# Top-k search packed into the query stage, ScalarE's exponential and ids parted, transposes in the norms, weights split three units ahead

## The chip, the core and the metric

The kernel runs on one core of one Trainium2 chip. The metric is the device time of one execution in microseconds; of several executions the median is taken. A core has TensorE (PE; PEld is its weight load), the vector engine (DVE), ScalarE (ACT), GpSimd (POOL) and SyncE (SP, which here only issues DMAs). Each engine works through its own list of instructions in order and waits on semaphores.

## What is computed

A two-layer encoder over 256 tokens of width 1024, all in float32. Each layer is a token mixer (windowed attention in layer 0, spatial gating in layer 1) and a product-key expert mixer, each behind an RMS norm and added to the residual. The expert mixer is what the change touches:

```python
def peer(h, w_query, sub_keys, expert_down, expert_up):
    q = (x @ w_query).reshape(T, PEER_HEADS, 2, D_HALF)          # 8 heads
    s = jnp.einsum('thcd,hckd->thck', q, sub_keys)
    s1, i1 = lax.top_k(s[:, :, 0], 16)
    s2, i2 = lax.top_k(s[:, :, 1], 16)
    cand = s1[..., :, None] + s2[..., None, :]
    cidx = i1[..., :, None] * 128 + i2[..., None, :]
    top_s, pos = lax.top_k(cand.reshape(T, 8, 256), 16)
    idx = jnp.take_along_axis(cidx.reshape(T, 8, 256), pos, axis=-1)
    gate = jax.nn.softmax(top_s, axis=-1)
    a = gelu(einsum('cd,chkd->chk', x, expert_down[idx]))
    y = einsum('chk,chkd->cd', a * gate, expert_up[idx])
```

There are 128 x 128 = 16384 experts. The kernel does not gather their rows: it multiplies by all of them and uses a table of gates that is zero but for the chosen ones.

## The kernel before

**Units.** All weights are streamed through SBUF in units of 128 x 1024 floats (512 KB). SyncE loads unit n into `raw[n % 4]` once `split_lo(n - 4)` is done (L282). ScalarE rounds it to fp32r in `w_hi[n % 4]` (`split_hi`, L451) and the vector engine forms the rest in `w_lo[n % 4]` (`split_lo`, L674). TensorE multiplies with three products, hi x hi, lo x hi and hi x lo (L1154 to L1156). `split_hi(n)` waits until TensorE has used unit n - 4 (`used >= n - 3`). The split of a unit stands AHEAD = 2 units ahead of its use in every engine's program.

**Stages of a layer.** The mixer (20 units in layer 0, 72 in layer 1), a norm, the query stage (16 units), the down stage (128 units, `acts` = gelu of x times all experts' down rows), the up stage (128 units), and the residual. In the norm (`norm_turn`, L1186) TensorE transposes the scaled activations, ScalarE copies them to `x_hi` and the vector engine forms `x_lo`.

**The search.** An item is one head of one tile of 128 tokens, 16 items a layer. Its top-k runs on the vector engine in small steps that are placed by hand between the weight splits: `sides_first`, `sides_places`, `sides_second`, `sides_last` (top 16 of each half), `candidates`, `best_first` to `best_last` (top 16 of the sums), `best_parts`, `best_columns`, `best_hits`, `best_keys`, `best_experts` (ids in `chosen`, semaphore `found`), `same_*` (an expert that was chosen by an earlier head too), `totals` (the gate in `whole`, semaphore `gate_done`). In the query stage, iteration c of the vector engine is the split of unit c + AHEAD, a copy of the scores of unit c (which TensorE finishes behind unit c + 1) and the steps that stand under `if c == ...`. In the down stage every item has a slot of SLOT = 7 units; the slot of item m also holds the last steps of item m - 1. ScalarE does `exponentials(item)` (waits `shifted`, which `best_parts` sets) and `names(item)` (waits `found`, writes the scatter's addresses, sets `named`); it stands in its own loop behind the eviction of a unit. After the exponential it loads the Gelu table again (L600).

**The scatter.** GpSimd first clears the table `gates` in DRAM by 32 DMAs of zeros a layer (L370); in layer 0 the last 8 wait for the first 8 query units. Then it stores the gates by indirect DMAs, 16 an item and 256 a layer (L385):

```python
for m in range(ITEMS):
    pool.wait_ge(gate_done, ITEMS * layer + m + 1)
    pool.wait_ge(named, ITEMS * layer + m + 1)
    if head:
        pool.wait_ge(added[layer][t], 16 * TOPK * head)
    for k in range(TOPK):
        pool.indirect_dma_start(flat, ...)
```

**The up stage.** SyncE's order there is the load of up unit 0, then a wait until all stores of the layer have landed (`added`, L312), then the gates of column 0 into `g_t`, up unit 1, and so on. For each column the vector engine multiplies `acts` by `g_t` (`gate`, L1113), ScalarE rounds the product to `l_hi` (`operand_hi`, L639, which waits until TensorE has used the unit before the last), the vector engine forms `l_lo` (`operand_lo`, L1118), and TensorE uses both with the up unit (`rows`). In ScalarE's program `split_hi(up + c + AHEAD)` stands ahead of `operand_hi(c + 1)`. In the down stage it stands ahead of the eviction of column c (`evict`, L624).

## Time and profile before

| | before |
|---|---|
| median of 3 runs | 1984.69 us (1978.02 to 1987.01) |
| profiled execution, its own time | 1983.99 us |
| span of its instructions | 1982.2 us |
| mean granted TensorE clock | 0.98 |
| PE busy | 1878.9 us (95%) |
| DVE busy | 1376.1 us (69%) |
| ACT busy | 1009.6 us (51%) |
| POOL busy | 704.5 us (36%) |
| chain that ended last | PE 59%, POOL 26%, issue 8% |

The profile is of one execution. Times in its rows are microseconds from the first instruction; a granted clock of 1.00 is 2.4 GHz and 0.50 is 1.2 GHz. Matmul rows overlap, since their ends are modelled: the distance from start to start is the rate. In a timeline row "[2.49 <-DVE big L713]" says how long the engine had stood idle before the instruction and what released it. "xN" counts the instructions merged in a row.

### The profile page before, as it was taken

What the parts mean: (1) busy time and instruction counts of PE and PEld (TensorE: products, weight loads), DVE (VectorE), ACT (ScalarE), POOL (GpSimd) and SP (SyncE); (2) the same over time, 40 slices, a digit from 0 to 9 for tenths busy, and PEclk for the clock granted to TensorE, in tenths of its full rate; (3) what the DMA queues carried; (4) which work ended last, traced back from release to release, by engine and by line L of the source; (5) the groups of instructions that cost most, each with busy time, mean ns of one, the idle gap of its engine ahead of it and who ended that gap; (6) DMA issues with size and microseconds to landing.
All of it is one profiled execution on the core that took longest, in us unless ns stands there. A gap on an engine that the chain in (4) does not pass through costs nothing.

```text
span 1982.2 us, 38591 instructions
## 1 busy us (share of the span) xinstructions
PE 1878.9 (95%) x12066; PEld 1706.5 (86%) x12066; DVE 1376.1 (69%) x2944; ACT 1009.6 (51%) x1633; POOL 704.5 (36%) x628
## 2 busy tenths in 40 slices
PE   7989999999959999999999999999999959999998
PEld 6889999999958888887889989999999948888886
DVE  5857778887436667667577767778888427766666
ACT  5634565665435555555444445565565425555553
POOL 1314777888730000000102103778788740000000
PEclk9989999999979999999999999999999979999999
DMA  6974555545547778886849744545555537777775
GB/s 226 343 253 168 177 164 181 176 167 180 188 131 242 240 242 280 290 295 213 280 153 335 268 145 156 182 161 181 176 172 173 192 106 240 242 241 241 240 241 194
DMA packets 158145, 419.96 MB, mean 212 GB/s; under 512 B 32267, under 2 KB 65067, under 8 KB 157580
## 3 DMA queue, kind: packets, MB, share of 16 engines
q1 hardware_dynamic: 129116, 369.23, 56.5%
q0 software_dynamic: 28976, 50.17, 7.6%
q8 instruction: 16, 0.26, 0.1%
q14 instruction: 37, 0.30, 0.0%
HBM read 382.30 MB, written 37.00 MB: 212 GB/s over the span
## 4 chain that ended last, share of the span: by engine, by line
PE 59%; POOL 26%; issue 8%; ACT 2%; DVE 2%; DMA 2%; SPq 0%; DVEq 0%; POOLq 0%; ACTq 0%
POOL gates L385 26%; PE psum L1154 19%; PE psum L1156 19%; PE psum L1155 19%; DMA big<-bias_rows 1%; PE psum L1335 1%; ACT w_hi L451 1%; DVE w_lo L674 1%; PE psum L1312 1%; ACT L600 1%; DVE big L713 1%; ACT L598 0%; PE psum L1239 0%; PE psum L1265 0%; DMA raw<-in_up 0%
## 5 line engine op out<-in xcount | busy, mean ns | idle before, releaser
L674 DVE TENSOR_TENSOR w_lo<-raw,w_hi 128x1024 fp32r<-128x1024 f32 x636 | 772.0, 1219 | 257.7 <-ACT w_hi L451 256.9
L1154 PE MATMUL psum<-x_hi,w_hi 128*128 128x256 f32 x2576 | 739.8, 287 | 19.3 <-DVE w_lo L674 16.6
L1155 PE MATMUL psum<-x_lo,w_hi 128*128 128x256 f32 x2576 | 732.1, 284 | 0.0
L1156 PE MATMUL psum<-x_hi,w_lo 128*128 128x256 f32 x2576 | 731.8, 284 | 0.0
L385 POOL DMA_INDIRECT gates<-whole,address x512 | 629.1, 1229 | 253.4 <-issue 165.0
L451 ACT CAST w_hi<-raw 128x1024 fp32r<-128x1024 f32 x636 | 661.2, 1045 | 60.4 <-DMA raw<-in_up 49.9
L1154 PEld LDWEIGHTS psum<-x_hi,w_hi 128*128 128x128 f32 x2576 | 497.5, 193 | 30.0 <-issue 28.2
L1155 PEld LDWEIGHTS psum<-x_lo,w_hi 128*128 128x128 f32 x2576 | 497.9, 193 | 0.9
L1156 PEld LDWEIGHTS psum<-x_hi,w_lo 128*128 128x128 f32 x2576 | 497.5, 193 | 0.0
L1154 PE MATMUL psum<-w_hi,l_hi 128*128 128x512 f32 x1152 | 453.5, 394 | 45.7 <-DVE l_lo L1118 44.6
L1156 PE MATMUL psum<-w_hi,l_lo 128*128 128x512 f32 x1152 | 450.2, 391 | 0.0
L1155 PE MATMUL psum<-w_lo,l_hi 128*128 128x512 f32 x1152 | 450.1, 391 | 0.0
L1154 PEld LDWEIGHTS psum<-w_hi,l_hi 128*128 128x128 f32 x1152 | 217.5, 189 | 90.5 <-issue 46.4
L639 ACT CAST l_hi<-big 128x256 fp32r (+1 forms) x256 | 104.1, 406 | 336.7 <-PE psum L1156 333.1
L624 ACT ACTIVATE big<-psum 128x256 f32<-128x256 f32 x256 | 97.9, 382 | 324.7 <-PE psum L1156 324.7
L1156 PEld LDWEIGHTS psum<-w_hi,l_lo 128*128 128x128 f32 x1152 | 217.3, 189 | 45.9
L1155 PEld LDWEIGHTS psum<-w_lo,l_hi 128*128 128x128 f32 x1152 | 217.5, 189 | 44.7
L1118 DVE TENSOR_TENSOR l_lo<-big,l_hi 128x256 fp32r<-128x256 f32 x256 | 109.0, 426 | 211.1 <-ACT l_hi L639 210.9
L437 POOL DMA_DIRECT2D big<-h_kept x4 | 2.2, 554 | 366.4 <-PE psum L1156 366.4
L370 POOL DMA_DIRECT2D gates<-zeros x64 | 48.3, 756 | 198.0 <-PE psum L1156 188.3
L1113 DVE TENSOR_TENSOR big<-big,g_t 128x256 f32 (+1 forms) x256 | 107.1, 419 | 2.9 <-DMA g_t<-gates 2.8
L425 POOL DMA_DIRECT2D big<-in_ln_g x4 | 2.2, 549 | 209.3 <-PE psum L1156 209.3
(134 smaller groups left out, 1116.4 us busy)
## 6 DMA issues: line engine op xcount, KB each, us to landing
raw<-in_down SPq DMA_DIRECT2D x256, 512.0 KB
raw<-in_up SPq DMA_DIRECT2D x256, 512.0 KB
raw<-in_sg_units SPq DMA_DIRECT2D x72, 512.0 KB
gates<-zeros POOLq DMA_DIRECT2D x64, 512.0 KB, 6.2
g_t<-gates SPq DMA_DIRECT2D x256, 128.0 KB, 3.7
raw<-in_query SPq DMA_DIRECT2D x32, 512.0 KB
raw<-in_attn_units SPq DMA_DIRECT2D x20, 512.0 KB
gates<-whole,address POOLq DMA_INDIRECT x512
```

What stands on the lines that cost most here:

```text
L370: pool.dma_start(gates[layer][ZERO_UNITS * q:ZERO_UNITS * q + ZERO_UNITS].rearrange("i p t -> p i t"), zeros[:, :].rearrange("p (o t) -> p ...
L385: pool.indirect_dma_start(flat, bass.IndirectOffsetOnAxis(address[:, TOPK * m + k:TOPK * m + k + 1], 0), whole[:, t, head, k:k + 1], None, ...
L451: act.copy(w_hi[n % SPLIT][:, :], raw[n % RAW][:, :]).then_inc(hi_done, 1)
L600: act.preload_act_table(ACT.Gelu_apprx_tanh)
L624: act.activation(acts[:, bass.ds(i * group + n, 1), :], p1[n % 2].rearrange("p (o t) -> p o t", o=1), ACT.Gelu_apprx_tanh).then_inc(p1_rea ...
L639: act.copy(l_hi[n % 2][:, :].rearrange("p (o t) -> p o t", o=1), acts[:, bass.ds(i * GROUP + n, 1), :]).then_inc(l_hi_done, 1)
L674: dve.tensor_tensor(w_lo[n % SPLIT][:, :], raw[n % RAW][:, :], w_hi[n % SPLIT][:, :].bitcast(F32), ALU.subtract).then_inc(lo_done, 1)
L1113: dve.tensor_tensor(a, a, g_t[n % G_TILES][:, :].rearrange("p (o t) -> p o t", o=1), ALU.mult).then_inc(gated_up, 1)
L1118: dve.tensor_tensor(l_lo[n % 2][:, :].rearrange("p (o t) -> p o t", o=1), acts[:, bass.ds(i * GROUP + n, 1), :], l_hi[n % 2][:, :].bitcast ...
L1154: pe.matmul(out_ap, hi_s, hi_m, start=start, stop=False)
L1155: pe.matmul(out_ap, hi_s, lo_m, start=False, stop=False)
L1156: return pe.matmul(out_ap, lo_s, hi_m, start=False, stop=stop)
```

## The change

It makes six edits.

1. AHEAD goes from 2 to 3: every split, in all stages, is placed one unit earlier against TensorE's use.
2. In the query stage the steps are packed. Item 0's gate (`totals(0)`) goes from iteration 13 to 7, item 1's from the down stage to iteration 12, and item 2's search is done up to `best_columns`. Item 3's sides are started in iteration 15 and finished in the first two units of the down stage. The slots of the down stage begin at unit 2 (SLOTS_FROM) with item 3 (FIRST_ITEMS), and end at unit 100 and not 105.
3. On ScalarE `exponentials` and `names` are parted: in the query stage they stand behind units 7 and 8 for item 0, and 12 and 13 for item 1; in a slot, behind its first and third unit.
4. The Gelu table is no longer loaded in `exponentials` but behind it, and not between items 0 and 1.
5. The second, third and fourth `norm_turn` begin with FILL = 26 transposes of old `x_lo` columns into PSUM bank 7, and nothing reads what they write. They wait for nothing.
6. A tile `iota` that nothing used is gone, so `made` counts to 7 and not to 8 (those lines are left out below).

```diff
--- before.py
+++ after.py
@@ -33,7 +33,10 @@
 CAND = WIDE * TOPK + (TOPK - WIDE) * NARROW
 HALF = NK // 2
 SLOT = 7
+SLOTS_FROM = 2
+FIRST_ITEMS = 3
 ZERO_UNITS = 4
+FILL = 26
 G_TILES = 4
 RMS_EPS, LN_EPS = 1e-6, 1e-5
 MASKED = -1.0e30
@@ -44,7 +47,7 @@
 GROUP = 4
 RAW = 4
 SPLIT = 4
-AHEAD = 2
+AHEAD = 3
 ATTN_UNITS, SG_V_UNITS, SG_UNITS, QUERY_UNITS = 20, 24, 72, 16
 MIX_UNITS = (ATTN_UNITS, SG_UNITS)
 SG_LOADS = 16
...
@@ -597,7 +596,6 @@
                     act.wait_ge(shifted, ITEMS * layer + item + 1)
                     act.activation(vals[:, item % 2, :], top1[:, item % 2, :], ACT.Exp, bias=least[:, item % 2:item % 2 + 1],
                                    accum_out=sums[:, item % 2:item % 2 + 1]).then_inc(exp_done, 1)
-                    act.preload_act_table(ACT.Gelu_apprx_tanh)
 
                 def names(item):
 
@@ -613,10 +611,15 @@
                     split_hi(u["query"] + c + AHEAD)
                     act.wait_ge(used, u["query"] + c + 1)
                     act.copy(q_p[c % 2], p1[c % 2]).then_inc(p1_read, 1)
-                    if c == 9:
+                    if c == 7:
                         exponentials(0)
+                    if c == 8:
+                        names(0)
                     if c == 12:
-                        names(0)
+                        exponentials(1)
+                        act.preload_act_table(ACT.Gelu_apprx_tanh)
+                    if c == 13:
+                        names(1)
 
                 def evict(n, i=0, group=GROUP):
 
@@ -624,12 +627,16 @@
                     act.activation(acts[:, bass.ds(i * group + n, 1), :], p1[n % 2].rearrange("p (o t) -> p o t", o=1),
                                    ACT.Gelu_apprx_tanh).then_inc(p1_read, 1)
 
-                for n in range(SLOT * (ITEMS - 1)):
+                searched = SLOTS_FROM + SLOT * (ITEMS - FIRST_ITEMS + 1)
+                for n in range(searched):
                     split_hi(u["down"] + n + AHEAD)
                     evict(n)
-                    if n % SLOT == 2:
-                        exponentials(n // SLOT + 1)
-                        names(n // SLOT + 1)
+                    item = (n - SLOTS_FROM) // SLOT + FIRST_ITEMS - 1
+                    if n >= SLOTS_FROM and (n - SLOTS_FROM) % SLOT == 0:
+                        exponentials(item)
+                        act.preload_act_table(ACT.Gelu_apprx_tanh)
+                    if n >= SLOTS_FROM and (n - SLOTS_FROM) % SLOT == 2:
+                        names(item)
 
                 def operand_hi(n, i=0):
 
@@ -639,7 +646,7 @@
                     act.copy(l_hi[n % 2][:, :].rearrange("p (o t) -> p o t", o=1),
                              acts[:, bass.ds(i * GROUP + n, 1), :]).then_inc(l_hi_done, 1)
 
-                for n in range(SLOT * (ITEMS - 1), NK):
+                for n in range(searched, NK):
                     if n == SCORES_COLUMN:
                         act.wait_ge(search_done, layer + 1)
                         act.wait_ge(h_stored, 16 * (layer + 1))
...
@@ -1016,55 +1023,72 @@
                                     pg[c % 2][:, 0:T].rearrange("p (t n) -> p t n", t=TT)).then_inc(s_read, 1)
                     if c == 2:
                         a = sides_first(0)
+                        a = sides_places(0, a)
                     if c == 3:
-                        a = sides_places(0, a)
-                    if c == 4:
                         a = sides_second(0, a)
                         a = sides_last(0, a)
+                        b = candidates(0, a)
+                    if c == 4:
+                        b = best_first(0, b)
+                        b = best_places(0, b)
+                        b = best_second(0, b)
+                        b = best_last(0, b)
                     if c == 5:
-                        b = candidates(0, a)
-                        a = sides_first(1)
-                    if c == 6:
-                        b = best_first(0, b)
-                        a = sides_places(1, a)
-                    if c == 7:
-                        b = best_places(0, b)
-                        a = sides_second(1, a)
-                    if c == 8:
-                        b = best_second(0, b)
-                        a = sides_last(1, a)
-                        b = best_last(0, b)
-                    if c == 9:
                         b = best_parts(0, b)
                         b = best_columns(b)
+                        e = best_hits(b)
+                    if c == 6:
+                        e = best_keys(e)
+                        best_experts(e)
+                    if c == 7:
+                        totals(0, None)
+                        a = sides_first(1)
+                        a = sides_places(1, a)
+                    if c == 8:
+                        a = sides_second(1, a)
+                        a = sides_last(1, a)
+                        b = candidates(1, a)
+                    if c == 9:
+                        b = best_first(1, b)
+                        b = best_places(1, b)
+                        b = best_second(1, b)
+                        b = best_last(1, b)
                     if c == 10:
-                        b = best_hits(b)
-                        b = best_keys(b)
+                        b = best_parts(1, b)
+                        b = best_columns(b)
+                        e = best_hits(b)
                     if c == 11:
-                        best_experts(b)
-                        b = candidates(1, a)
+                        e = best_keys(e)
+                        best_experts(e)
                         a = sides_first(2)
                     if c == 12:
-                        b = best_first(1, b)
+                        totals(1, None)
                         a = sides_places(2, a)
                     if c == 13:
-                        totals(0, None)
-                        b = best_places(1, b)
+                        a = sides_second(2, a)
+                        a = sides_last(2, a)
+                        b = candidates(2, a)
                     if c == 14:
-                        b = best_second(1, b)
-                        a = sides_second(2, a)
-                        b = best_last(1, b)
+                        b = best_first(2, b)
+                        b = best_places(2, b)
+                        b = best_second(2, b)
+                        b = best_last(2, b)
                     if c == 15:
-                        b = best_parts(1, b)
-                        a = sides_last(2, a)
+                        b = best_parts(2, b)
                         b = best_columns(b)
+                        a = sides_first(3)
 
                 def low(n):
 
                     split_lo(u["down"] + n + AHEAD)
 
-                for item in range(2, ITEMS + 1):
-                    n = SLOT * (item - 2)
+                a = sides_places(3, a)
+                low(0)
+                a = sides_second(3, a)
+                a = sides_last(3, a)
+                low(1)
+                for item in range(FIRST_ITEMS, ITEMS + 1):
+                    n = SLOTS_FROM + SLOT * (item - FIRST_ITEMS)
                     now, more = item < ITEMS, item + 1 < ITEMS
                     e = best_hits(b)
                     if now:
@@ -1103,7 +1127,8 @@
                     if now:
                         b = best_columns(b)
                 dve.sem_inc(search_done, 1)
-                for n in range(SLOT * (ITEMS - 1), NK):
+
+                for n in range(SLOTS_FROM + SLOT * (ITEMS - FIRST_ITEMS + 1), NK):
                     low(n)
 
                 def gate(n, i=0):
@@ -1185,6 +1210,9 @@
 
             def norm_turn(z):
 
+                if z:
+                    for k in range(FILL):
+                        pe.transpose(psum[:, 7, P * (k % 4):P * (k % 4) + P], x_lo[:, k % KD, 0:P].bitcast(F32), ident[:, :])
                 for t in range(TT):
                     pe.wait_ge(scaled_done, TT * z + t + 1)
                     for k in range(KD):
```

## Rows read from the trace of the kernel before

**Rows 1.** The page, chain that ended last, share of the span by engine.
```profile
PE 59%; POOL 26%; issue 8%; ACT 2%; DVE 2%; DMA 2%; SPq 0%; DVEq 0%; POOLq 0%; ACTq 0%
```

**Rows 2.** Windows: stretch, length, busy PE, PEld, DVE, ACT, POOL, clock, DMA share, GB/s.
```profile
120.00:173.00 53.00, 51.48 (x424) 50.53 (x424) 32.82 (x101) 21.88 (x37) 7.35 (x9) 1.00 0.64 219
173.00:556.00 383.00, 374.55 (x3080) 370.39 (x3078) 281.92 (x739) 217.50 (x360) 304.25 (x248) 1.00 0.52 172
556.00:576.00 20.00, 0.14 (x2) 0.00 (x0) 2.40 (x5) 2.27 (x4) 8.02 (x9) 0.61 0.36 113
```

**Rows 3.** Waits: engine and line, waited for whom: us, times, longest.
```profile
POOL gates L385 <- DVE whole L1006: 87.8, 2, 60.9
...
PE psum L1154 <- DVE l_lo L1118: 44.6, 2, 24.7
```

**Rows 4.** Timeline, first gate, first and last store of layer 0, first of layer 1.
```profile
170.60 0.23 DVE L1006 TENSOR_SCALAR whole<-vals,sums 128x16 f32<-128x16 f32 x1
...
171.69 1.97 POOL L385 DMA_INDIRECT gates<-whole,address  x1 [26.91 <-DVE whole L1006]
...
565.50 0.96 POOL L385 DMA_INDIRECT gates<-whole,address  x1 [0.30 <-issue]
...
1214.46 2.03 POOL L385 DMA_INDIRECT gates<-whole,address  x1 [60.89 <-DVE whole L1006]
```

**Rows 5.** Timeline of ACT: query units 0, 8, 12, ids; layer 1's unit 8.
```profile
120.67 0.37 ACT L615 COPY big<-psum 128x256 f32<-128x256 f32 x1 [3.04 <-PE psum L1156]
...
148.10 0.37 ACT L615 COPY big<-psum 128x256 f32<-128x256 f32 x1 [3.03 <-PE psum L1156]
...
163.42 0.37 ACT L615 COPY big<-psum 128x256 f32<-128x256 f32 x1 [2.96 <-PE psum L1156]
...
163.93 0.30 ACT L609 ACTIVATE address<-big,token 128x16 uint32<-128x16 f32 x1
...
1189.33 0.37 ACT L615 COPY big<-psum 128x256 f32<-128x256 f32 x1 [3.16 <-PE psum L1156]
```

**Rows 6.** Source L370, the clear issued at 144.03.
```profile
DMA to landing us min/median/max: 5.0/5.0/5.0
```

**Rows 7.** Windows around two norms, columns as in rows 2.
```profile
115.50:120.00 4.50, 4.44 (x21) 4.47 (x22) 3.40 (x7) 2.13 (x5) 0.00 (x0) 0.50 0.00 0
...
926.70:929.50 2.80, 0.01 (x1) 0.00 (x0) 2.45 (x7) 1.18 (x4) 1.63 (x2) 0.91 0.52 180
929.50:932.40 2.90, 2.87 (x14) 2.87 (x15) 0.75 (x1) 0.43 (x2) 0.01 (x1) 0.50 0.00 0
```

**Rows 8.** Timeline of PE, four transposes at the full clock.
```profile
59.85 0.60 PE L1239 MATMUL psum<-ident,big 128*128 128x128 f32 x4
```

**Rows 9.** Source L385 in 500 to 550, then in 556 to 567: ns min/median/max.
```profile
L385 POOL DMA_INDIRECT gates<-whole,address x35: 954/1151/1320, 499.4 to 549.6; - x35
...
L385 POOL DMA_INDIRECT gates<-whole,address x9: 954/958/959, 555.4 to 565.5; - x9
```

**Rows 10.** Timeline of SP's queue, ACT and PE, handoff of layer 0.
```profile
568.07 0.42 SPq L282 DMA_DIRECT2D raw<-in_up  x1
...
569.01 0.43 SPq L282 DMA_DIRECT2D raw<-in_up  x1
...
572.39 1.04 ACT L451 CAST w_hi<-raw 128x1024 fp32r<-128x1024 f32 x1 [18.70 <-DMA raw<-in_up]
...
576.07 0.77 PE L1154 MATMUL psum<-w_hi,l_hi 128*128 128x512 f32 x1 [19.93 <-DVE l_lo L1118]
```

**Rows 11.** Timeline of ACT, second weight split of the program.
```profile
9.64 1.05 ACT L451 CAST w_hi<-raw 128x1024 fp32r<-128x1024 f32 x1 [0.81 <-DMA raw<-in_attn_units]
```

**Rows 12.** Timeline of DVE, residual behind layer 0's up stage.
```profile
924.79 2.65 DVE L713 TENSOR_TENSOR big<-psum,big 128x512 f32<-128x512 f32 x4 [0.29 <-PE psum L1156]
```

**Rows 13.** Timeline of ACT and DVE, one unit of the up stage.
```profile
703.80 0.41 ACT L639 CAST l_hi<-big 128x256 fp32r x1 [1.36 <-PE psum L1156]
...
704.24 0.43 DVE L1118 TENSOR_TENSOR l_lo<-big,l_hi 128x256 fp32r<-128x256 f32 x1 [0.82 <-ACT l_hi L639]
```

12 lines of the change are left out of this document (4 added, 8 removed).

## The prediction

> **What bounds the kernel now.** I read the chain that ended last first, because a busy share averages over stages with different limits. TensorE and GpSimd's indirect stores at L385 divide that chain [rows 1]. The windows by stage say where. In a down stage TensorE is busy 374.55 of 383 us, so its own rate nearly sets the length. Then it does nothing for 20.0 us, while the vector engine and ScalarE do 2.4 and 2.3 us of work and GpSimd goes on scattering [rows 2]. The waits put this idle time and layer 1's, which is 24.7 us (44.6 us together), down to the first `l_lo` of the up stage. They also show that GpSimd waited for a gate only twice in 512 stores, once a layer, before the first store [rows 3]. So the search does not pace the scatter. From its first store at 171.69 to the end of its last at 566.46, 394.8 us, it never lacks work [rows 4]: 256 stores at 1.54 us. A scatter that starts x earlier ends x earlier, and until 20 us are won the up stage starts x earlier. What makes the down stage itself faster moves nothing; it only lengthens TensorE's wait. The change has to be read in this order: what starts the scatter, what its stores cost, what follows the last one.
>
> **Start of the scatter.** Item 0's first store needs `gate_done`, `named` and the cleared `gates`. Today the gate is computed in iteration 13 of the query stage and the ids named in iteration 12. After the change they are computed in iterations 7 and 8. What ends last then? ScalarE's names(0) run right behind the copy of unit 8. Before, that copy began at 148.10, and unit 12's at 163.42 with the last of the three id activations ending at 164.23, so 0.8 us behind that copy's start [rows 5]. If nothing else moved, the ids would be ready at 148.9. The vector engine must have the gate by then. Work for one item is, from the trace, about 7 us (the sixteen iterations hold 32.8 us of vector work [rows 2], of which 16 x (1.13 + 0.34) = 23.5 us are weight splits and score copies; the 9.3 us left hold all of item 0 and half of items 1 and 2, with waits between dependent steps outside the busy time). Packed, each iteration holds 1.47 us of split and copy and 1.6 to 1.7 us of search, 3.1 to 3.2 us in all, against 3.39 us for a TensorE unit here (27.43 us from unit 0's copy to unit 8's, over 8, gives 3.43 [rows 5]). It fits with little room, and the third split unit covers an iteration that overruns. Following the new order from iteration 2 on gives the gate of item 0 about 3.9 us after unit 7's end, ahead of the names. The cleared `gates`: the last clear is issued at 144.03, behind unit 7, and lands 5.0 us later [rows 6], so 0.4 us behind the names at most. From readiness to the first store the trace shows 0.86 us (gate computed at 170.60 in 0.23 us, store at 171.69 [rows 4]).
>
> **The clock and the fill.** TensorE's granted clock is 0.50, its lower level of 1.2 GHz, from 115.5 to 120.0, the first query unit of layer 0 [rows 7], and so it is in layer 1; before that TensorE had stood idle for the norm. 26 transposes at the full clock take 26 x 0.107 = 2.8 us (four take 0.60 us with 0.27 us of pipeline behind the last [rows 8]), no more than the idle time of the tightest of the three norms, 2.8 us between the layers [rows 7]; the other two have 3.5 and 3.8. They wait for nothing and so cost nothing, and if the clock stays at its upper level, the first query unit is paced by `x_lo` instead: it ends 0.8 us behind the last `x_lo`. The norm's sixteen transposes end sooner too. Together that is 3.0 us earlier in layer 0 (1.0 of it from the transposes), 2.1 us in layer 1 by the same reckoning (its transposes began at the full clock), and 0.9 us at the norm between the layers. Do fp32 transposes hold the clock? In 929.5 to 932.4 TensorE ran transposes alone, at the lower level, and from 932.4 on it stood at the upper one [rows 7]. Here transposes raised it. The Trainium skill says otherwise ("TensorE: Matmul & The Clock Gate", Part 4, PE-mode transpose: transposes do not count as TensorE activity for the clock in the same way). By that rule of the Trainium skill the fill would be worth nothing and the sum 6.0 us higher; the trace disagrees with it at 932.4. I go by the trace, with a doubt that is priced as a rival.
>
> **Start of the scatter, summed.** Layer 0: unit 8 ends 3.0 earlier, at 145.1; names at 145.9; first store at 146.8, 24.9 us earlier. Layer 1: unit 8's copy began at 1189.33 [rows 5]; less 2.1, plus 0.8 and 0.86, gives 1188.9, plus 0.4 (below) against 1214.46 [rows 4], 25.2 us earlier. The Exp table in layer 1 is loaded behind unit 7's copy and is done (1.28 + 0.5 us) before unit 8 ends.
>
> **Cost of a store.** With the vector engine idle a store takes 0.96 us, all nine from 556 to 567; behind the search, with one weight split a unit, they range from 0.95 to 1.32 [rows 9]. So one split costs the scatter 0.36 us. Starting five query units earlier, it meets 5 more splits, 1.8 us, and one more item's search, about 1 us (bounds 0 and 3). Items 0 and 1 took 48.2 us together, and item 2's gate comes about 48.5 us after the first store (15 units at 2.88 to 3.4 us, and 3.1 us of split and steps), so a short wait of 0 to 1.5 us appears; I take 0.7. Sum 3.5 us a layer, bounds 1 and 10 (the upper end: items 0 and 1 at 1.7 us a store, the dearest item's mean of 27.4 us). The Trainium skill ("SBUF — State Buffer", Who interferes with whom) infers that `tensor_tensor` does not hold up descriptor generation; by it this term would be 0.7 us, and the trace disagrees by its 0.36 us a split.
>
> **Handoff to the up stage.** SyncE stands behind the `added` wait with only up unit 0 loaded. Unit 1 was issued at 568.07 and landed for ScalarE at 572.39; then split, the last eviction, both gates and `l_hi`, `l_lo` led to TensorE at 576.07, 3.7 us later [rows 10]. With AHEAD 3, ScalarE must also split up unit 2 before it evicts column 127, and unit 2 is issued at 569.01. By bytes (1.3 MB at some 300 GB/s) it lands at about 573.8. So +1.4 us a layer, bounds 0.9 (the issue alone) and 3.
>
> **What else AHEAD moves.** At the start a third split stands ahead of the copy of the bias row and of `x_hi`. The second began at 9.64 after a wait of 0.81 for its weights [rows 11], and the third's land about 1.6 us behind it (0.5 MB at some 340 GB/s): +1.7 us, bounds 1.0 and 3, since bias_rows goes on to DMA and to the first scores. At the end of layer 0's up stage the last split now waits for unit 126 and ends at about 926.3, so the residual starts there and not at 924.79 [rows 12]: +1.4 us, less 0.9 for the clock, +0.5. At the end of the gating stage the same costs 0.4. In the up stage ScalarE's split (1.05 us) now waits for the same unit as `l_hi` and goes first. `l_lo` started 0.44 us behind `l_hi` (703.80, 704.24) and takes 0.43; with the split ahead it is ready 1.9 us after the unit's end, where 2.72 us are to be had [rows 13]. Covered, so nothing; without that cover each 0.1 us late would be 25.6 us over 256 units.
> The 15 slots of each down stage lose 0.55 to 0.8 us each to ScalarE's two table loads (8.4 us of idle TensorE in 383 [rows 2]); the third unit hides them. It wins 8 to 12 us a layer for TensorE and nothing for the end, because the scatter ends later. Dropping `iota` (0.25 us of GpSimd at the start) is behind the DMA of `x`: nothing.
>
> **Sum.** Start +1.7. Layer 0: -24.9 + 3.5 + 1.4 = -20.0. Between layers +0.5. Layer 1: -25.2 + 3.5 + 1.4 = -20.3. Together -38.1 us. The profiled execution took 1983.99 us (span 1982.2 and 1.8 around it), 0.7 below the median of 1984.69: 1983.99 - 38.1 = 1945.9, rounded 1946. TensorE would still idle 17 us in layer 0 (down stage ends at 539.4, up starts at 556.1, both less the 1.7) and about 21 us in layer 1.
>
> **Rivals.** (1) The fill does not hold the clock: the first query units stay at the lower level, +3.0, +2.1, +0.9 = 1952. Against it stands 932.4 [rows 7]; for it, some idle time remains behind the fill and behind the norm's transposes. The Trainium skill's rule on transposes, named above, is this case. (2) The scatter slows: the vector engine is nearly full from iteration 2 on, every split and search step holds up stores, and item 2's gate is just late. +6 us a layer: 1958. (3) The packed search overruns: if an iteration takes over 3.43 us on average, the third unit's reserve is gone after a few, TensorE stalls and the first store slips by some iterations. Losing half of the advance gives 1971. (4) Less contention than I charge and a handoff that costs nothing: 1938. (5) The other side: `l_lo` in the up stage. Behind the split it has 0.8 us of room. From 2.72 us on TensorE waits in each of 256 units; at 0.15 us beyond, the whole gain is eaten, at 0.2 us a unit it ends at 1946 + 51 = 1997. The 1.9 us from [rows 13] speak against it. (6) The change does not do what it says: the clears or another wait hold the first store where it was, and the extra unit's costs remain, 1984 + 5 - 6 = 1983.
>
> **Chances.** Forecast 0.52 (own range 1940 to 1950), rival 1 0.18, rival 2 0.11, rival 3 0.05, rival 4 0.06, rival 5 0.05, rival 6 0.03. Faster than before by over 0.5% (about what a measurement here can tell from no change) in all but rivals 5 and 6: 0.92, of which I move 0.02 to no change for what I have not seen; same 0.05, slower 0.05. The range takes in the forecast and rivals 1, 2 and 4: 1936 to 1960.
>
> **What would show it.** First store at about 148.5 in layer 0 (146.8 + 1.7) with its wait ending on the names; stores without idle time but for item 2; the clock at its upper level through the norms; no 0.55 us gaps in the down stage; TensorE idle 17 and 21 us before the up stages, ended by `l_lo`; up units still 2.72 us. A first store behind 155 us, gaps in the query stage, or up units over 2.8 us would make the prediction wrong.

## The result and the profile after

The changed kernel took 1965.40 us (median of 4, 1962.08 to 1965.82), the kernel before in the same comparison 1985.85 us (4 runs): a ratio of 0.9896, 95% interval 0.986 to 0.9932. The forecast was 1946 us, in 1936 to 1960, so the time lies above the range. The change won 20 us and not 38. The profiled execution took 1965.82 us, with a span of 1963.7 us.

In four of the later comparisons the kernel before itself took 2239 to 2291 us (medians); no execution time from those is used in the argument.

The chain that ended last, of the page of the changed kernel, answers to [rows 1]:

```profile
PE 58%; POOL 28%; issue 8%; DMA 2%; DVE 1%; ACT 1%; SPq 0%; DVEq 0%; POOLq 0%; ACTq 0%
```

GpSimd's share has grown from 26 to 28%. The windows of the down stage of layer 0 and of the two idle times before the up stages, in the columns of [rows 2]:

```profile
173.00:541.00 368.00, 368.00 (x3069) 368.00 (x3068) 276.28 (x708) 214.53 (x349) 292.47 (x227) 1.00 0.58 177
541.30:569.70 28.40, 0.00 (x0) 0.00 (x0) 3.63 (x6) 3.60 (x6) 13.40 (x14) 0.55 0.27 93
...
1576.90:1606.00 29.10, 0.00 (x0) 0.00 (x0) 3.65 (x6) 3.62 (x6) 13.41 (x14) 0.59 0.27 90
```

TensorE now has 368.00 us of work in 368 of down stage: the gaps of the slots are gone. It then stands idle for 28.4 and 29.1 us, where it was 20.0 and 24.7. The third unit ahead did for TensorE what it should and the end got nothing of it, as forecast; but the waits were to shrink to 17 and 21 us. The waits of the changed kernel, as in [rows 3]:

```profile
POOL gates L384 <- issue: 168.6, 510, 3.9
...
PE psum L1179 <- DVE l_lo L1143: 57.7, 2, 29.2
...
POOL gates L384 <- ACT address L607: 35.3, 1, 35.3
...
POOL gates L384 <- DMA gates<-zeros: 5.1, 1, 5.1
```

The up stages wait for `l_lo` for 57.7 us in all. GpSimd waits for another engine or a DMA only ahead of its first store of a layer (for the clears in layer 0, for the ids in layer 1). Under "issue" the row also holds two pauses a layer, of 3.3 to 3.9 us, before the 113th and the 225th store (at 338.0 and 517.7 in layer 0). The kernel before has them at the same two stores, 1.7 to 4.0 us long. What they wait for the profile doesn't name. The first and last stores of both layers, timeline, which answer to [rows 4]:

```profile
149.82 1.63 POOL L384 DMA_INDIRECT gates<-whole,address  x1 [5.09 <-DMA gates<-zeros]
...
557.85 0.96 POOL L384 DMA_INDIRECT gates<-whole,address  x1 [0.31 <-issue]
...
1184.92 1.74 POOL L384 DMA_INDIRECT gates<-whole,address  x1 [35.31 <-ACT address L607]
...
1593.41 0.96 POOL L384 DMA_INDIRECT gates<-whole,address  x1 [0.30 <-issue]
```

The first store of layer 0 is 21.9 us earlier, the last one only 7.6 (565.50 to 557.85). The scatter took 409.0 us in layer 0 and 409.4 in layer 1, where it had taken 394.8 and 399.9. A store's mean length rose from 1.225 and 1.233 us in the two layers to 1.268 and 1.270. In layer 0 that makes 11.0 us, and the two pauses another 3.2; in layer 1 it makes all of the 9.5.

From the two traces, each term of the sum against what it measured (positions of the first or last store, of TensorE's first product of a stage, and of the ends of spans):

| term | forecast | measured |
|---|---|---|
| start (TensorE's last attention unit, 104.72 to 107.96) | +1.7 | +3.2 |
| first store, layer 0, against that | -24.9 | -25.1 |
| scatter, layer 0 | +3.5 | +14.2 |
| handoff (end of the last store to TensorE), layer 0 | +1.4 | +1.3 |
| up stage, residual, norm | +0.5 | +0.8 |
| gating stage to first store, layer 1 | -25.2 | -24.0 |
| scatter, layer 1 | +3.5 | +9.5 |
| handoff, layer 1 | +1.4 | +2.3 |
| up stage of layer 1 to the end | 0 | -0.8 |
| sum | -38.1 | -18.6 |

The measured column adds up to the difference of the spans, 1982.2 - 1963.7 = 18.5. Of the 19.5 us that are missing, 16.7 lie in the scatter. Each column of positions is one execution.

### The profile page after: what moved, and what is told of

Same layout as the page of the kernel before. It is cut to its first block, busy times and chain, and to the rows that moved or that the text cites. A ratio compares the mean times of both kernels' runs of the same rounds, so it can differ in the third digit from the quotient of the medians.

```text
span 1963.7 us, 38730 instructions
## 1 busy us (share of the span) xinstructions
PE 1869.4 (95%) x12144; PEld 1706.1 (87%) x12144; DVE 1381.6 (70%) x2944; ACT 1006.9 (51%) x1629; POOL 725.0 (37%) x627
## 4 chain that ended last, share of the span: by engine, by line
PE 58%; POOL 28%; issue 8%; DMA 2%; DVE 1%; ACT 1%; SPq 0%; DVEq 0%; POOLq 0%; ACTq 0%
POOL gates L384 28%; PE psum L1179 18%; PE psum L1181 18%; PE psum L1180 18%; DMA big<-bias_rows 1%; PE psum L1363 1%; PE psum L1340 1%; DMA raw<-in_up 1%; DVE big L720 1%; PE psum L1267 0%; PE psum L1256 0%; PE psum L1293 0%; DMA raw<-in_attn_units 0%; ACT w_hi L450 0%; POOL stat L356 0%
## 5 line engine op out<-in xcount | busy, mean ns | idle before, releaser
L384 POOL DMA_INDIRECT gates<-whole,address x512 | 649.8, 1269 | 209.0 <-issue 168.6
L1179 PE MATMUL psum<-w_hi,l_hi 128*128 128x512 f32 x1152 | 453.4, 394 | 58.7 <-DVE l_lo L1143 57.7
```

The lines of the kernel that those rows point to most:

```text
L384: pool.indirect_dma_start(flat, bass.IndirectOffsetOnAxis(address[:, TOPK * m + k:TOPK * m + k + 1], 0), whole[:, t, head, k:k + 1], None, ...
L1179: pe.matmul(out_ap, hi_s, hi_m, start=start, stop=False)
```

## Why the scatter became slower: a first look

One stretch of the changed kernel's down stage, stores first, then the vector engine's steps with two SBUF operands (`tensor_tensor`) that ran beside them:

```profile
224.12 0.96 POOL L384 DMA_INDIRECT gates<-whole,address  x1 [0.30 <-issue]
225.38 0.96 POOL L384 DMA_INDIRECT gates<-whole,address  x1 [0.30 <-issue]
...
228.50 1.91 POOL L384 DMA_INDIRECT gates<-whole,address  x1 [0.30 <-issue]
...
232.41 2.53 POOL L384 DMA_INDIRECT gates<-whole,address  x1 [0.30 <-issue]
```

```profile
226.14 1.23 DVE L681 TENSOR_TENSOR w_lo<-raw,w_hi 128x1024 fp32r<-128x1024 f32 x1 [2.86 <-ACT w_hi L450]
...
228.36 1.22 DVE L681 TENSOR_TENSOR w_lo<-raw,w_hi 128x1024 fp32r<-128x1024 f32 x1
...
232.31 1.20 DVE L681 TENSOR_TENSOR w_lo<-raw,w_hi 128x1024 fp32r<-128x1024 f32 x1
233.43 0.68 DVE L994 TENSOR_TENSOR big<-big,whole 128x512 f32<-128x512 bf16 x1
...
234.52 1.23 DVE L681 TENSOR_TENSOR w_lo<-raw,w_hi 128x1024 fp32r<-128x1024 f32 x1
```

At 224.12 the vector engine has no step of the kind and the store takes 0.96 us. The store at 228.50 begins inside the split of 228.36 to 229.58 and takes 1.91. The one at 232.41 meets a split and the product of L994 back to back and takes 2.53. So a store's price is no constant 0.36 us per split; it hangs on where in the store the step falls and on what follows without a gap.

The traces let one say more. The split that began at 226.14, inside the store of 225.38, cost that store nothing. The two long stores end 0.83 us behind the end of the step, or of the row of steps without a gap, that ran when they began: 229.58 + 0.83 = 230.41, and 234.11 + 0.83 = 234.94. Of the 274 stores of the changed kernel that took over 1.0 us, 271 end 0.83 us behind the end of such a step, and in the kernel before 263 of 266. A split that begins after the store has begun leaves it at 0.96 us, 122 times in the changed kernel. So a store waits at its start, if such a step is running then, and not later.

**Theory A.** A store stops while the vector engine runs steps with two SBUF operands. Putting the splits one unit further ahead takes away the pauses in which stores ran free, so the same vector work costs more stores' time. **Theory B.** The early start in a crowded query stage and the new places of the steps make the scatter dearer, whatever AHEAD is. **Rival C**, tried later: any busy vector engine, or the streamed loads, slow the stores.

## Experiments

**AHEAD alone, undone and done.** Two kernels:

```diff
 # after_ahead2: the changed kernel
-AHEAD = 3
+AHEAD = 2
 # before_ahead3: the kernel before
-AHEAD = 2
+AHEAD = 3
```

> The changed kernel with AHEAD back at 2, all else as changed. Theory A (spacing): a store's cost hangs on how the vector engine's long two-input steps fall against it, and splitting three units ahead is what moved that from 14 to 12 stores in a 7-unit slot; then the scatter here takes about 395 to 400 us a layer (after: 409), the handoff 9.6 us (after: 11.0 and 11.7), the start loses 3 us less, and the time is about 1965 - 22 - 3 - 3 = 1937 us. Theory B (early start): the scatter is dearer because it begins in the crowded query stage and the steps of the slots were placed anew, whatever AHEAD is; then the scatter stays at 405 to 410 us and only start and handoff come back: about 1959 us. A third outcome, TensorE or the vector engine stalling in the query stage for want of the third unit, would show as a later first store (over 152 us).

Measured: 1944.35 us, ratio to before 0.9793 (0.9774 to 0.9812), that is 21 us below the changed kernel, which was measured in another comparison. The scatter takes 401.4 us in both layers (147.21 to 548.60 in layer 0). The handoff is 9.4 and 9.6 us, the first store comes 2.6 us earlier, and the query stage did not suffer. Windows of the down stage and of the two idle times:

```profile
173.00:545.80 372.80, 370.08 (x3054) 366.96 (x3052) 276.36 (x705) 216.01 (x351) 295.56 (x237) 1.00 0.57 175
545.80:558.00 12.20, 0.05 (x1) 0.00 (x0) 2.42 (x5) 2.29 (x4) 2.19 (x3) 0.70 0.58 194
1570.90:1583.10 12.20, 0.00 (x0) 0.00 (x1) 2.44 (x5) 2.31 (x4) 2.06 (x3) 0.65 0.57 207
```

The idle times are 12.2 us each. Most of the scatter's excess is gone: 409.2 us on average fell to 401.4, 7.8 less a layer, and a slot of seven units takes 20.53 us where it took 20.16. What stays against an average of 397.3 before is 4.1 us, near the 3.5 that the early start was priced at. Between the two traces, 22.1 us apart, 15.6 are the two scatters, 2.6 the start and 3.6 the two handoffs. Theory A had put the scatter at 395 to 400 us and Theory B at 405 to 410: the result lies just above A's range.

> The kernel before with AHEAD 3 and nothing else. Theory A: the 7-unit slots shrink from 20.96 to 20.16 us, stores per slot fall from 14 to 12 or 13, the scatter takes 405 to 410 us instead of 395 and 400; with +3 us at the start, +1.4 and +2 at the handoffs the time is about 1985 + 12 + 3 + 3 = 2003 us, though TensorE loses no time in the down stages. Theory B: the scatter keeps 395 to 400 us and the time is about 1991 us.

Measured: 1995.83 us, ratio 1.0044 (1.0028 to 1.0061): AHEAD 3 by itself makes the kernel slower by 9 us. But its scatter takes 398.8 and 399.0 us (394.8 and 399.9 before), as Theory B said, and not 405 to 410. TensorE's idle times before the up stages:

```profile
543.00:582.70 39.70, 0.01 (x1) 0.03 (x1) 3.69 (x6) 3.66 (x6) 21.06 (x22) 0.55 0.21 67
...
1598.50:1637.20 38.70, 0.01 (x1) 0.04 (x1) 3.71 (x6) 3.68 (x6) 21.08 (x22) 0.55 0.20 68
```

They are 39.7 and 38.7 us long, because in layer 0 TensorE ends its down stage 13 us earlier, while the scatter begins at 171.8 as before and ends 4 us later, and the handoff is 12.1 us and not 9.6. Stores in 220 to 420 us, the same 200 us of the down stage, in four kernels (before, changed, after_ahead2, before_ahead3), ns as min/median/max:

```profile
L385 POOL DMA_INDIRECT gates<-whole,address x129: 954/1118/2536, 218.7 to 418.8; - x129
```

```profile
L384 POOL DMA_INDIRECT gates<-whole,address x121: 954/1217/2935, 219.6 to 419.8; - x121
```

```profile
L384 POOL DMA_INDIRECT gates<-whole,address x123: 954/1179/2935, 219.7 to 418.5; - x123
```

```profile
L385 POOL DMA_INDIRECT gates<-whole,address x124: 955/1128/2872, 219.2 to 419.3; - x124
```

AHEAD 3 took the kernel before from 129 to 124 stores in that time. Over the two layers its scatter still grew by only 3 us. One part of that is seen: the down stage ended 27.6 us ahead of the end of the last store (10.3 before), and behind it stores cost 1.26 us from start to start and not 1.6. I estimate that at 5 us: the 17.3 us more of such a tail hold 13.7 stores, which at 1.6 us would take 22. Where the rest was won back isn't shown. Neither theory was right as put: AHEAD costs the scatter 7.8 us a layer in the new arrangement and next to nothing in the old one. Differences of 2 or 3 us a layer say little here, since `after_ahead2` and `ahead2_loads_first_3`, which have the same program up to the last store on all engines but SyncE, differ by 3.0 us in layer 1 (401.4 and 404.4).

**What a store waits for.** In the changed kernel the subtraction of each split (but for the first four units of each straight-line part) is replaced by a step that takes as long but reads one SBUF operand (and writes half as many elements). The low parts of the weights are left out of the result.

```diff
-dve.tensor_tensor(w_lo[n % SPLIT][:, :], raw[n % RAW][:, :], w_hi[n % SPLIT][:, :].bitcast(F32), ALU.subtract)
+dve.tensor_reduce(w_lo[n % SPLIT][:, 0:D // 2], raw[n % RAW][:, :].rearrange("p (n k) -> p n k", k=2), AX.X, ALU.add)
```

> The changed kernel with each weight split's subtraction replaced by a tensor_reduce of one SBUF operand (low parts of the weights left out), again, on a chip where the kernel before takes its usual 1985 us. Theory A (a store stops while a two-operand step of the vector engine runs): stores behind the search take 0.96 us, the scatter falls from 409 to 325 to 350 us a layer and the time to 1905 to 1920 us. Rival C (any busy vector engine, or the loads, slow the stores): scatter over 395 us, time about 1960 us.

Measured: 1907.39 us, in one execution. Stores in the same 200 us, and windows of the down stage and of what is left of the idle time before the up stage:

```profile
L384 POOL DMA_INDIRECT gates<-whole,address x152: 954/958/1934, 219.5 to 419.9; - x152
```

```profile
173.00:541.70 368.70, 368.69 (x3072) 368.48 (x3071) 278.59 (x715) 216.77 (x353) 238.21 (x238) 1.00 0.61 184
541.70:543.00 1.30, 0.00 (x0) 0.03 (x1) 0.95 (x4) 1.28 (x3) 0.00 (x0) 1.00 0.07 5
```

152 stores and not 121, with a median of 958 ns; the scatter takes 346.7 and 348.5 us; the vector engine is as busy as before (278.59 us of the stage) and the loads run as fast. Rival C is out. The run alone doesn't tell whether the second operand counts or the number of elements written, since the new step also writes half as many. The traces do: in nine of them (both kernels and the seven runs of this section outside its last table) a store began 142 times while a MATCH_REPLACE8 step ran, which reads one SBUF operand and writes as many elements as it reads, and none of these stores was lengthened. In this run 48 stores still take over 1.0 us, and 45 of them end 0.83 us behind another `tensor_tensor` step. Of the scatter's 346.7 and 348.5 us, 322 are 256 stores at 1.26 us, 10 and 13 are such longer stores, and 14 are pauses, 8 and 9 of them before the first store of item 2, whose gate now comes too late. With the scatter off the chain, TensorE waits 1.3 us before the up stage and its clock stays at the upper level.

**Shorter steps.** AHEAD 2, and each split's subtraction in two steps of 512 columns (indices shortened):

```diff
-dve.tensor_tensor(w_lo[:, :], raw[:, :], w_hi[:, :], ALU.subtract).then_inc(lo_done, 1)
+for b in range(2):
+    c = slice(D // 2 * b, D // 2 * b + D // 2)
+    ins = dve.tensor_tensor(w_lo[:, c], raw[:, c], w_hi[:, c], ALU.subtract)
+ins.then_inc(lo_done, 1)
```

> The changed kernel with AHEAD 2 and each split's subtraction in two steps of 512 columns, on a chip where the kernel before takes 1985 us. If a store waits for the running step alone: scatter 380 to 390 us a layer (401 with whole splits), time about 1920 us. If it waits until the vector engine has a pause: 1944 to 1950 us.

Measured: 1944.59 us, ratio 0.9774 (0.9747 to 0.9801), the same as with whole splits (0.9793); scatter 402.5 and 400.1 us.

```profile
L384 POOL DMA_INDIRECT gates<-whole,address x126: 952/1137/3006, 219.2 to 419.8; - x126
```

126 stores against 123 in that stretch, and nothing in the whole. The time is the one expected if a store waited until the vector engine has a pause, but the trace shows another reason. Of 89 stores that began inside the first half of a split, 60 ended 0.83 us behind that half and only 29 later, so a store mostly waits for the running half alone. One stretch with one split a unit, stores and then splits:

```profile
521.77 1.32 POOL L384 DMA_INDIRECT gates<-whole,address  x1 [0.31 <-issue]
523.39 0.96 POOL L384 DMA_INDIRECT gates<-whole,address  x1 [0.30 <-issue]
524.65 1.31 POOL L384 DMA_INDIRECT gates<-whole,address  x1 [0.30 <-issue]
```

```profile
520.96 1.29 DVE L683 TENSOR_TENSOR w_lo<-raw,w_hi 128x512 fp32r<-128x512 f32 x2 [1.59 <-ACT w_hi L450]
```

The store meets the second half and still waits 0.36 us, as with whole splits. Two stores take 2.52 us and a unit 2.88, so I take it that the stores drift against the splits until one of them meets a step late enough to lose just 0.36, whether the step is whole or halved. In all, the waits fell by 3.8 us a layer and the pauses between stores grew by 3.7.

**The handoff.** AHEAD 2, and all four buffers loaded before SyncE waits for the stores:

```diff
+for c in range(GROUP):
+    load(u["up"] + c, up_units[layer][:, bass.ds(c * D, D)], 0)
+
 def up_unit(c, i):
-    load(u["up"] + c, up_units[layer][:, bass.ds((i * GROUP + c) * D, D)], i)
+    if not isinstance(i, int):
+        load(u["up"] + c, up_units[layer][:, bass.ds((i * GROUP + c) * D, D)], i)
```

> The changed kernel with AHEAD 2 and up units 0 to 3 loaded before SyncE waits for the stores, on a chip where the kernel before takes 1985 us. Handoff 6.3 us and not 9.5: about 1938 us. If landing of the gates and the chain behind it take the time anyway: 1944 us.

Measured: 1935.73 us, ratio 0.9723 (0.9702 to 0.9743), the fastest version that keeps the whole computation; ahead of the changed kernel's 1965.40 by 30 us. Last store, gates' issue, and TensorE's first product of the up stage (timelines of POOL, SP and PE):

```profile
549.34 0.95 POOL L388 DMA_INDIRECT gates<-whole,address  x1 [0.30 <-issue]
...
551.54 1.75 SPq L321 DMA_DIRECT2D g_t<-gates  x4
...
555.06 0.77 PE L1183 MATMUL psum<-w_hi,l_hi 128*128 128x512 f32 x1 [7.85 <-DVE l_lo L1147]
```

The handoff is 4.8 us (550.29 to 555.06), 4.8 in layer 1 too, and not the 6.3 that was expected. The same edit with AHEAD 3 is among the runs that decide little, below.

**The fill.** The changed kernel without it, and the kernel before with it:

```diff
 # after_nofill: the changed kernel
-FILL = 26
+FILL = 0
 # before_fill: the kernel before, in norm_turn
+if z:
+    for k in range(26):
+        pe.transpose(psum[:, 7, P * (k % 4):P * (k % 4) + P], x_lo[:, k % KD, 0:P].bitcast(F32), ident[:, :])
```

> The changed kernel without the 26 transposes in the norms (FILL 0). If they hold the clock, the first unit behind each norm runs at 0.50 again here and the time rises by 3 to 6 us, to about 1970. If the clock stayed up for another reason (where the norm falls in time), it stays within 1 us of 1965.

> The kernel before with the 26 transposes at the start of norms 2, 3 and 4 and nothing else. If they hold the clock by themselves: granted clock 1.00 at the three norms, time 4 to 6 us less, about 1980. If they do not count as work for the clock: no difference.

Measured: without it 1971.36 us (ratio 0.9919, 0.9901 to 0.9937), 6.0 more than the changed kernel (4.6 by the two ratios to the kernel before, as the comparisons differ). With it alone 1982.50 against 1986.79 (0.9981, 0.9969 to 0.9994), 4.3 less. Windows of the norm's transposes and the first query unit in after_nofill, then of fill, transposes and first units in before_fill, clock in the third column from the end:

```profile
115.70:119.90 4.20, 3.64 (x16) 3.24 (x16) 1.69 (x4) 1.80 (x6) 0.27 (x1) 0.50 0.61 253
119.90:125.00 5.10, 5.01 (x23) 5.04 (x24) 3.42 (x7) 2.15 (x5) 0.00 (x0) 0.50 0.09 21
```

```profile
107.60:111.00 3.40, 2.78 (x26) 2.54 (x24) 2.65 (x7) 1.54 (x4) 1.61 (x3) 1.00 0.63 202
111.00:115.00 4.00, 2.66 (x22) 2.46 (x23) 2.51 (x7) 2.59 (x8) 0.36 (x2) 1.00 0.64 262
115.00:120.00 5.00, 5.00 (x43) 4.97 (x42) 2.64 (x5) 2.69 (x5) 0.76 (x1) 1.00 0.26 56
```

In after_nofill the clock is 0.50 where the changed kernel, of which it differs by the fill alone, has 1.00 (below); in before_fill it is 1.00 where the kernel before had 0.50 [rows 7]. It is the fill's transposes that keep the clock. In before_fill the stretches from TensorE's last product ahead of a norm to its fiftieth behind it are 2.9, 1.1 and 2.0 us shorter than in the kernel before, where 3.0, 0.9 and 2.1 were forecast.

**Runs that decide little.** They ran in the four comparisons in which the kernel before took over 2230 us. They are the edits above and two more (`after_loads_first`: the changed kernel with the four loads first; `after_half_stores`, `half_stores_2`: the changed kernel with every second store left out).

> The changed kernel with the low half of each weight split replaced by a tensor_reduce over the raw unit (from the fifth unit of each straight-line part and in all loops): the vector engine is as long busy, but reads one SBUF operand and not two. It leaves the low part of the weights out of the result. Theory A (a store stops while a long two-operand step of the vector engine runs, so the spacing of the splits sets its cost): stores behind the search all take 0.96 us (after: 0.95 to 1.32), a layer's scatter takes 322.6 us + what the search costs, 340 to 365 us (after: 409), and TensorE's wait before the up stage falls to a few us: about 1915 us. Rival C (the stores are slowed by any busy vector engine, or by DMA traffic of the streamed weights): the scatter stays above 395 us.

> The changed kernel with AHEAD 2 and the split's subtraction done as two steps of 512 columns. If a store waits for the running step alone, its wait is at most half as long: the scatter falls from 401 to 380 to 390 us a layer and the time from 1944 to about 1920 us. If a store waits until the vector engine has a pause, nothing changes but some 0.07 us more per split: 1944 to 1950 us.

> The changed kernel with AHEAD 2 and the loads of up units 0 to 3 issued before SyncE waits for the stores, so only the gates of column 0 stand between the last store and the up stage. The handoff from the last store to TensorE falls from 9.5 to about 6.3 us a layer: 1944 - 6.5 = 1938 us. If the landing of the gates and the chain gate, l_hi, l_lo is what takes the time anyway: 1944.

> The changed kernel with 8 of 16 stores per item; it leaves half of the gates out. If the scatter alone sets the two waits before the up stages, both vanish (28.5 and 29.2 us) and with them the lower clock behind them (2.6 us each): 1965 - 60 = about 1905 us. If something else then ends last before the up stage, a wait of several us remains and names it.

> The same kernel as in after_reduce_split (changed kernel, each weight split's subtraction replaced by a tensor_reduce of one SBUF operand, low parts of the weights left out), again, since there the kernel before itself took 2274 us and TensorE stood waiting for loads. There its stores took 0.96 us but for 0.3 us in all of a layer. Theory A: here too the stores take 0.96 us each, so a layer's scatter falls from 409 to 325 to 350 us, is done before the down stage ends or soon behind it, and the time is 1905 to 1920 us. Rival C (any busy vector engine, or the loads, slow the stores): scatter over 395 us.

> The same kernel as in ahead2_halves (changed kernel, AHEAD 2, each split's subtraction in two steps of 512 columns), again on another chip. If a store waits for the running step alone: scatter 380 to 390 us a layer (401 with whole splits), time about 1920 us. If a store waits until the vector engine has a pause: 1944 to 1950 us.

> The same kernel as in ahead2_loads_first (changed kernel, AHEAD 2, up units 0 to 3 loaded before SyncE waits for the stores), again on another chip. Handoff 6.3 us and not 9.5: about 1938 us. If landing of the gates and the chain behind it take the time anyway: 1944 us.

> The same kernel as in after_half_stores (changed kernel with 8 of 16 stores per item, half of the gates left out), again on another chip. If the scatter alone sets the waits before the up stages (28.5 and 29.2 us), they vanish and the time is about 1905 us; what is left of a wait names the next bound.

> The changed kernel as it is (AHEAD 3) with up units 0 to 3 loaded before SyncE waits for the stores. If the longer handoff of the changed kernel (11.0 and 11.7 us from the last store to TensorE) comes only from up unit 2 being loaded behind the wait, it falls to the 4.8 us that AHEAD 2 has with the same order, 13 us in all, and the time is about 1952 us, still 16 us above AHEAD 2 for the slower scatter (409 us a layer) and the later start. If the third split costs on ScalarE or the vector engine there, the handoff stays above 6 us. If the order of the loads also changes the scatter, it leaves 409 us.

> The same kernel as in after_loads_first (AHEAD 3, up units 0 to 3 loaded before SyncE waits for the stores), again, where the kernel before takes its usual 1985 us. If only the load of up unit 2 lengthened the handoff: handoff 4.8 us, scatter 409 us, about 1952 us. If the third split costs more there: handoff over 6 us.

| run | us | kernel before beside it |
|---|---|---|
| after_reduce_split | 2434.07 | 2274.36 |
| reduce_split_2 | 2424.70 | 2291.39 |
| ahead2_halves | 2308.41 | 2274.36 |
| ahead2_halves_2 | 2294.28 | 2291.39 |
| ahead2_loads_first | 2270.68 | 2274.36 |
| ahead2_loads_first_2 | 2282.68 | 2291.39 |
| after_half_stores | 2040.54 | 2274.36 |
| half_stores_2 | 2046.59 | 2291.39 |
| after_loads_first | 2265.32 | 2281.14 |
| after_loads_first_2 | 2220.05 | 2239.53 |

None of the expected times came, and none can be held against them: the kernel before itself is 250 to 305 us longer here than in every other comparison. What made it so is open. The traces show where it lies: in reduce_split_2 ScalarE stands idle some 15.5 us once in every slot, before the first eviction behind the Gelu load (254.6, 291.4, 328.6 and so on), while TensorE issues single products with gaps that the profile puts under "issue". It isn't the length of the stores, since the reduce_split runs, whose stores are short, are the longest. But it seems to hang on how many there are: the two runs with half of the stores are over 230 us shorter than the kernel before beside them, where taking the scatter off the chain was worth 82 us in reduce_split_3, and ScalarE's longest stops there are 4.3 to 4.9 us. That reduce_split took 1907.39 us in the one undisturbed run and 2424.70 and 2434.07 here says that its time rests on a single execution; the length of its stores doesn't, as their median is 0.96 us in all three. Whether the early loads help with AHEAD 3 wasn't settled. With half of the stores TensorE waits 1.3 us before either up stage, so the scatter is then off the chain.

## Why the prediction was wrong, point by point

**Bound and its reading: right.** The scatter, from its first store on, set the start of both up stages; closing TensorE's gaps won nothing by itself: with AHEAD 3 alone the down stage of layer 0 is 13 us shorter and the kernel 9 us slower. That the scatter "never lacks work" is not quite so, as it has the two pauses a layer named above.

**Start of the scatter: right.** -24.9 forecast and -25.1 measured in layer 0, -25.2 and -24.0 in layer 1. The gate came 3.7 us behind unit 7's copy (3.9 forecast), the names 0.8 us behind unit 8's. The sign that the first wait ends on the names came true in layer 1 only: in layer 0 the last clear, issued at 143.97, took 5.6 us to land, 0.8 us behind the names (0.4 at most forecast). No wait came at item 2, for which 0.7 us were summed: items 0 and 1 took 51.1 us and not 48.2, and its gate was ready 2.3 us before. With AHEAD 2 the wait is 2.2 us. A TensorE unit is given once as 3.39 us and once as 3.43 in that working; nothing hangs on it. In layer 1 a gap of 3.5 us in the gating stage, which had passed at the upper level before, was followed by 3.4 us at the lower one, about 1.7 us. So rivals (3) and (6) are out: the packed search fits, and the first store moved.

**Fill and clock: right (rival 1 is out).** 6.0 us were forecast, and the runs gave 4.3 (before_fill) and 4.6 to 6.0 (after_nofill). The norm of layer 0 in the changed kernel, fill, transposes and first query unit, answers to [rows 7]:

```profile
110.90:114.00 3.10, 2.89 (x27) 2.65 (x25) 2.72 (x7) 1.65 (x4) 1.57 (x3) 1.00 0.79 254
114.00:117.30 3.30, 1.97 (x16) 1.73 (x16) 1.80 (x5) 1.85 (x6) 0.41 (x2) 1.00 0.76 315
117.30:120.00 2.70, 2.65 (x21) 2.65 (x22) 2.70 (x7) 2.11 (x5) 0.00 (x0) 1.00 0.04 12
```

The Trainium skill's rule that transposes do not count for the clock in the same way ("TensorE: Matmul & The Clock Gate", Part 4, PE-mode transpose) is not borne out by these runs, in which 26 of them kept the granted clock at 1.00.

**Cost of a store: the step that failed.** I had taken "one split costs the scatter 0.36 us" from the stretch behind the search, where one split a unit meets two stores a unit, and summed +3.5 us (bounds 1 and 10). Measured +14.2 and +9.5, where rival (2), whose mechanism it is, had 9.5 a layer (3.5 + 6). The rate of that stretch was a beat of two regular sequences (2 x 1.26 + 0.36 = 2.88, one unit), not the price of a split: a store that begins early in a split waits for nearly all of its 1.22 us, and for what follows without a gap as well. Along with it fell the sentence that what makes the down stage faster moves nothing: AHEAD 3 pressed the same vector work into slots of 20.16 us where AHEAD 2 has 20.53 (the kernel before 20.96), and this cost the scatter about 8 us a layer in the new arrangement (409.2 against 401.4). The other 4.1 us are near the 3.5 of the term, in sum and not part by part. That the two-operand steps lengthen the stores is shown by reduce_split_3, where the scatter falls from 409 to 348 us, and by the stores' ends. With AHEAD 3 there are hardly more long stores (274 for 270), but they wait longer, 159 us in all over both layers and not 146, and a slot has 12.0 stores on average and not 12.5. Why the starts then fall earlier into the steps was not worked out. The Trainium skill ("SBUF — State Buffer", Who interferes with whom) says that a vector step with two SBUF inputs contends with GpSimd instructions that read SBUF, and infers that descriptor generation is not held up by it. Here a store waits for such a step at its start, which 121 stores in 200 us against 152 show, and the 0.83 us behind that are not lengthened. What a store reads at its start no trace shows. Rival (4), less contention, is out with it.

**Handoff: right in layer 0** (+1.3 for +1.4), short by 0.9 in layer 1. Timeline of SP's queue, ACT and PE, as in [rows 10]:

```profile
561.36 0.43 SPq L284 DMA_DIRECT2D raw<-in_up  x1
...
566.08 1.04 ACT L450 CAST w_hi<-raw 128x1024 fp32r<-128x1024 f32 x1 [0.23 <-DMA raw<-in_up]
...
569.76 0.76 PE L1179 MATMUL psum<-w_hi,l_hi 128*128 128x512 f32 x1 [28.48 <-DVE l_lo L1143]
```

**Start: mis-sized.** +3.2 for +1.7. Timeline of ACT, the third split and the bias row's copy:

```profile
11.25 1.05 ACT L450 CAST w_hi<-raw 128x1024 fp32r<-128x1024 f32 x1 [0.20 <-DMA raw<-in_attn_units]
12.20 0.57 ACT L478 COPY big<-psum 16x512 f32<-16x512 f32 x1
```

The copy is 1.6 us later than before (10.60), as forecast. Behind it the vector engine came to the first scores 2.0 us later (34.83 for 32.81), and TensorE, idle for longer, then stood 6.8 us at the lower clock and not 3.4, which cost the rest.

**Up stage: right.** The split now goes ahead of `l_hi`, as in this unit, which answers to [rows 13]:

```profile
703.10 1.06 ACT L450 CAST w_hi<-raw 128x1024 fp32r<-128x1024 f32 x1 [1.36 <-PE psum L1181]
704.06 0.40 ACT L646 CAST l_hi<-big 128x256 fp32r x1
...
704.61 0.42 DVE L1143 TENSOR_TENSOR l_lo<-big,l_hi 128x256 fp32r<-128x256 f32 x1 [0.94 <-ACT l_hi L646]
```

`l_lo` is ready at 705.03, 1.9 us behind the unit's end; units still take 2.72 us. Rival (5) is out.

With AHEAD 2 the kernel lands at 1944 us, near the 1946 of the forecast. That is not the forecast come true: that sum had the third unit's costs in it and lacked those of the spacing.

## What to carry to other kernels

When GpSimd's indirect stores set the end, the vector engine's two-operand steps are part of their length, and a change that only makes the other engines tighter can lengthen them: price such stores by their count over a long stretch, with and without the steps, not by one regular stretch, and look at which step runs when a store begins. Splitting further ahead is worth nothing when the stage it smooths is not what ends last, and its costs at the start and at handoffs stay. Loads that do not depend on a wait belong ahead of it in SyncE's queue.

## What the runs showed of the hardware

An indirect store of 128 gates takes 0.96 us with 0.30 between stores. If the vector engine is in a step with two SBUF operands when the store begins, the store ends 0.83 us behind that step, or behind the row of such steps that follows without a gap (271 of 274 long stores in the changed kernel, the longest 4.0 us); a step that begins later leaves it at 0.96. Steps with one SBUF operand (`tensor_reduce`, `match_replace`) never lengthened one by themselves. Cutting a 1.22 us step in two back-to-back ones did not shorten the scatter. Float32 transposes of 128 x 128 held TensorE's granted clock at its upper level over a norm's 3 us, where idling let it fall.
